# Seven products instead of eight in both up projections of a two-block kernel, with two weight sums formed in SBUF

## What is computed

```python
# first block
h = rms_norm(x, norm2_g[layer])
gate, val = jnp.split(h @ w_up[layer], 2, axis=-1)
gate = jax.nn.silu(causal_depthwise_conv(gate, ffn_dw_w[layer], ffn_dw_b[layer]))   # 3 taps over the tokens
x = x + (gate * val) @ w_down[layer]
# second block
v = rmsnorm(h, norm_ffn_w[l])
gate = causal_depthwise_conv_2(v @ w_gate[l], conv_w[l], conv_b[l])                   # 3 taps over the tokens
h = h + (jax.nn.silu(gate) * (v @ w_up[l])) @ w_down[l]
```

## Time and profile before

| | us |
|---|---|
| median of 3 runs | 1204.06 |
| the profiled execution | 1203.35 |
| its span | 1201.5 |
| TensorE busy | 1169.1 (97%) |
| VectorE busy | 688.9 (57%) |
| ScalarE busy | 560.1 (47%) |
| GpSimd busy | 531.6 (44%) |
| up projection of the first block, quads 2 to 11 | 254.4 to 472.0 |
| up projection of the second block, ten sevenfold blocks | 870.9 to 1072.4 |

### The profile page before, as it was taken

One profiled execution on the slowest core, in us unless ns is written; L12 is line 12 of the kernel. 1 busy time (PEld: TensorE's weight loads), 2 busy tenths in 40 slices (PEclk: granted clock), 3 DMA queues, 4 the chain that ended last, 5 costly groups with the idle time before them and its releaser, 6 DMA issues.

```text
span 1201.5 us, 17233 instructions
## 1 busy us (share of the span) xinstructions
PE 1169.1 (97%) x6948; PEld 976.3 (81%) x6948; DVE 688.9 (57%) x979; ACT 560.1 (47%) x881; POOL 531.6 (44%) x288
## 2 busy tenths in 40 slices
PE   7999999999999998999999999999899999999997
PEld 6877768788888886888877767778799999998886
DVE  5999973343332334444574577865956666674444
ACT  6356575333232323232445565655566665652323
POOL 3540033655545454445684220008445555564443
PEclk9999999999999998999989999999999999999999
DMA  5422021268978968867823120213255555642321
GB/s 181 140 78 96 4 70 35 71 231 226 236 242 207 243 234 209 201 243 203 207 57 113 64 71 28 80 37 106 70 169 182 182 187 178 191 162 83 105 89 70
DMA packets 115672, 167.75 MB, mean 140 GB/s; under 512 B 3363, under 2 KB 95882, under 8 KB 115594
## 3 DMA queue, kind: packets, MB, share of 16 engines
q1 hardware_dynamic: 102634, 120.26, 30.2%
q0 software_dynamic: 12800, 46.14, 16.0%
q10 hardware_dynamic: 160, 0.26, 0.1%
HBM read 164.29 MB, written 48.23 MB: 177 GB/s over the span
## 4 chain that ended last, share of the span: by engine, by line
PE 88%; DVE 5%; ACT 3%; issue 1%; POOL 1%; DMA 1%; POOLq 0%; ACTq 0%; DVEq 0%; SPq 0%
PE ps L2294 16%; PE ps L1960 13%; PE ps L1962 13%; PE ps L1961 13%; PE ps L2351 10%; PE ps L2355 10%; PE ps L2049 4%; PE ps L2539 3%; PE ps L2095 1%; DVE act_t L1508 1%; PE ps L2491 1%; PE ps L2080 1%; ACT w_hi L744 1%; PE ps L2410 1%; PE ps L2446 1%
## 5 line engine op out<-in xcount | busy, mean ns | idle before, releaser
L610 POOL TENSOR_TENSOR w_lo<-w_raw,w_hi 128x1024 fp32r<-128x1024 f32 x176 | 445.2, 2532 | 518.2 <-ACT w_hi L744 517.3
L744 ACT ACTIVATE w_hi<-w_raw 128x1024 fp32r<-128x1024 f32 x220 | 231.7, 1055 | 278.7 <-PE ps L1962 84.5
L1960 PE MATMUL ps<-h_hi,w_hi 128*128 128x512 f32 x656 | 261.7, 399 | 3.0 <-DVE h_lo L1347 2.1
L1961 PE MATMUL ps<-h_lo,w_hi 128*128 128x512 f32 x656 | 255.7, 390 | 0.0
L1962 PE MATMUL ps<-h_hi,w_lo 128*128 128x512 f32 x656 | 255.7, 390 | 0.0
L1558 DVE TENSOR_TENSOR tt<-act_t,tt 128x512 fp32r<-128x512 f32 x44 | 97.8, 2232 | 117.1 <-ACT tt L971 117.1
L1960 PEld LDWEIGHTS ps<-h_hi,w_hi 128*128 128x128 f32 x656 | 123.1, 188 | 36.3 <-issue 7.5
L1962 PEld LDWEIGHTS ps<-h_hi,w_lo 128*128 128x128 f32 x656 | 123.1, 188 | 26.2
L1961 PEld LDWEIGHTS ps<-h_lo,w_hi 128*128 128x128 f32 x656 | 123.2, 188 | 24.5 <-issue 0.5
L1565 DVE TENSOR_TENSOR ps<-ps,rbs 128x512 f32<-128x512 f32 x88 | 61.5, 698 | 120.2 <-PE ps L1962 118.9
L2294 PE MATMUL ps<-tt,w_hi 128*128 128x256 f32 x640 | 116.2, 283 | 0.0
(11 more groups left out here) (331 smaller groups left out, 1949.3 us busy)
## 6 DMA issues: line engine op xcount, KB each, us to landing
w_raw<-in_w_up SPq DMA_DIRECT2D x23, 1024.0 KB, 6.9
w_raw<-in_w_down SPq DMA_DIRECT2D x22, 1024.0 KB, 4.9
w_raw<-blocks SPq DMA_DIRECT2D x40, 512.0 KB, 3.6
w_raw<-in_w_in SPq DMA_DIRECT2D x19, 1024.0 KB, 5.1
blocks<-in_w_up POOLq DMA_DIRECT2D x12, 1408.0 KB, 10.5
blocks<-in_w_gate POOLq DMA_DIRECT2D x12, 1408.0 KB, 6.3
blocks<-blocks POOLq DMA_DIRECT2D x8, 1408.0 KB, 10.4
w_raw<-in_w_gate SPq DMA_DIRECT2D x20, 512.0 KB, 3.6
```

Source lines behind the costliest of these rows:

```text
L610: pool.tensor_tensor(unit_view(w_lo, at, flat), unit_raw(at, flat), unit_view(w_hi, at, flat).bitcast(F32), ALU.subtract).then_inc(s_lo, 1)
L744: act.activation(unit_view(w_hi, at, flat), unit_raw(at, flat), ACT.Copy).then_inc(s_hi, 1)
L1960: pe.matmul(ps[:, bank, :], whi, hi, start=first, stop=False, skip_group_check=True)
L1961: pe.matmul(ps[:, bank, :], whi, lo, start=False, stop=False, skip_group_check=True)
```

## The change

Both blocks now have one quad and ten sevenfold blocks. The buffer `blocks` and its 32 transfers go. Of the seven weights of a block, five are loaded. Position 3 and 4 are formed on VectorE in a new buffer `sum_raw` from loaded ones (`half_sum`). Of the five loaded, two (the products 0 and 6) are sums of two quarters: SP loads one quarter into `w_raw`, and GpSimd issues a DMA that adds the other onto it (`added`). The first block of each layer takes its products in the order 1, 2, 0, 3 and so on. The crossed activations are formed from eight gained tiles `xg` by four operations of 1024 elements on VectorE, all behind the variance. The first four units of the down projection are loaded one by one, and its first two k tiles take six banks before the last two.

```diff
-NC = (11, 1)
+NC = (1, 1)
...
 def on_vector(u):
-    return block_of(u) is not None and block_of(u)[1] in (1, 3, 5)
+    at = block_of(u)
+    return at is not None and at[1] in (1, 3, 5) and at not in ((0, 1), (NS[0], 1))
...
+def is_sum(u):
+    at = block_of(u)
+    return at is not None and at[1] in (3, 4)
+LOADED = [u for u in range(U_END) if not is_sum(u)]
...
+FIRST_ORDER = (1, 2, 0, 3, 4, 5, 6)
+def product_order(i, lay):
+    return FIRST_ORDER if i == NC[lay] else tuple(range(NB))
...
+        sum_raw = sb("sum_raw", [P, 2, DM])
...
-        blocks = nc.dram_tensor("blocks", (4, DK, DFF), F32, kind="Internal").ap()
...
         # SP: one_block
+                n = LOAD_AT[u]
+                before = LOADED[n - 4]
+                wait_lo(sp, before)
...
+                if block_of(before) is not None:
+                    g, at = block_of(before)
+                    j = order_of(g)[at]
+                    if j < 3:
+                        sp.wait_ge(s_sum, 2 * g + (2 if j == 2 else 1))
...
+                    halves = {0: val[0, 0:DK, v], 1: gate[0, 0:DK, n], 2: gate[0, DK:DM, n],
+                              5: val[0, DK:DM, v], 6: val[0, 0:DK, v]}
+                    for at, j in enumerate(product_order(i, lay)):
+                        if j in halves:
+                            one_block(u + at, halves[j])
...
         # GpSimd, behind each residue
+                    if u + 1 in FIRST_BLOCK:
+                        added(u + 1 + FIRST_ORDER.index(0))
+                    if block_of(u) is not None:
+                        g, at = block_of(u)
+                        if at == 2:
+                            added(u + 4)
+                        if at == 4 and g % NS[0] < NS[0] - 1:
+                            added(u + 3)
+            def added(u):
...
+                src = gate[0, 0:DK, c0:c0 + 256] if j == 6 else val[0, DK:DM, v0 + c0:v0 + c0 + 256]
+                wait_landed(pool, u)
+                pool.dma_start(unit_raw(u, True).rearrange("p (k n) -> p k n", k=KH),
+                               src.rearrange("(k p) n -> p k n", p=P), accum_op=ALU.add).then_inc(s_add[j // 6], 16)
...
         # ScalarE, between the units of the output projection
+            def gained(m, gcol):
+                act.activation(xg[:, m, :], xT[:, m, :], ACT.Copy, scale=par[:, 0, gcol + m:gcol + m + 1]).then_inc(s_xg, 1)
...
         # VectorE
+            def cross(lay, n):
+                b11, b12 = xg[:, 0:KH, 0:NH], xg[:, 0:KH, NH:SEQ]
...
+                    dve.tensor_tensor(t1f, b11, b12, ALU.subtract).then_inc(s_tf, 1)
...
+                def half_sum(i, n):
...
+                    if n == 0:
+                        wait_raw(dve, s1)
+                        wait_raw(dve, a11)
+                        if i > NC[lay]:
+                            wait_lo(dve, u - NB + 3)
+                        dve.tensor_tensor(unit_raw(u + 3, True), unit_raw(s1, True), unit_raw(a11, True),
+                                          ALU.add).then_inc(s_sum, 1)
+                    else:
+                        dve.wait_ge(s_sum, 2 * g + 1)
+                        wait_raw(dve, a12)
+                        if i > NC[lay]:
+                            wait_lo(dve, u - NB + 4)
+                        dve.tensor_tensor(unit_raw(u + 4, True), unit_raw(u + 3, True), unit_raw(a12, True),
+                                          ALU.add).then_inc(s_sum, 1)
...
         # VectorE, sevenfold
                     rest(u + 3)
+                    rest(u + 5)
                     for c in range(2):
...
-                        joined(c, 2, q1c, 2, left, CROSS)
-                    rest(u + 5)
+                        joined(c, 2, q1c, q1_at, left, CROSS)
+                    if not last:
+                        half_sum(i + 1, 0)
+                        half_sum(i + 1, 1)
...
         # TensorE, down
-                for k in range(KF - 2):
-                    ktile(u0 + k, k, first=(k == 0))
+                for ms in (range(6), range(6, KD)):
+                    for k in range(2):
+                        ktile(u0 + k, k, ms, first=(k == 0))
+                for k in range(2, KF - 2):
+                    ktile(u0 + k, k, range(KD))
```

More of the change, by code:

```diff
@@ L2280, in stream, with product @@
                     return h_hi[:, at, half], h_lo[:, at, half]
[L2282 removed]
+                def product(at, j, c):
                     bank = (SUM, ROW, CROSS, ROW, SUM, CROSS, ROW)[j][c]
[L2285 removed]
+                    whi, wlo = (quarter(w[:, (u + at) % 4, :]) for w in (w_hi, w_lo))
                     for k in range(KH):
@@ L2296, in product, with ready @@
                     mm.then_inc(s_q, 1)
-                wait_lo(pe, u)
-                if first:
-                    pe.wait_ge(s_tl, crossed + 1)
-                for c in range(2):
-                    if first:
+                def ready(j, c):
+                    if j == 0 and first:
+                        pe.wait_ge(s_tl, crossed + 1)
                         pe.wait_ge(s_gv, tiles + c - 1)
-                    else:
+                    elif j == 0:
                         pe.wait_ge(s_c, 8 * (g - 1) + 2 + c + 1)
-                    product(0, c)
@@ L2307, in sevenfold @@
-                wait_lo(pe, u + 1)
-                for c in range(2):
-                    if first:
+                    if j == 1 and first:
                         pe.wait_ge(s_conv, tiles + c - 1)
-                    else:
+                    elif j == 1:
                         pe.wait_ge(s_c, 8 * (g - 1) + 4 + 2 * c + 2)
-                    product(1, c)
-                wait_lo(pe, u + 2)
-                for c in range(2):
-                    if first and lay:
-                        pe.wait_ge(s_tc, 8)
-                    if not first:
-                        pe.wait_ge(s_c, 8 * (g - 1) + 4 + 2 * c + 1)
-                    product(2, c)
@@ L2334, in sevenfold @@
-                for c in range(2):
-                    pe.wait_ge(s_c, 8 * g + c + 1)
-                    product(5, c)
-                wait_lo(pe, u + 6)
-                for c in range(2):
-                    pe.wait_ge(s_qc, 8 * g + 4 + c + 1)
-                    product(6, c)
+                    if j == 2 and first:
+                        pe.wait_ge(s_rbs, lay + 1)
+                        if lay:
+                            pe.wait_ge(s_tc, 8)
+                    elif j == 2:
+                        pe.wait_ge(s_c, 8 * (g - 1) + 4 + 2 * c + 1)
@@ new lines, in ready @@
+                    if j == 3:
+                        if first:
+                            pe.wait_ge(s_tl, crossed + 2)
+                        pe.wait_ge(s_qc, 8 * g + (0 if first else 2) + c + 1)
+                    if j == 4:
+                        pe.wait_ge(s_qc, 8 * g + (2 if first else 0) + c + 1)
+                    if j == 5:
+                        if first:
+                            pe.wait_ge(s_tl, crossed + 3)
+                        pe.wait_ge(s_c, 8 * g + c + 1)
+                    if j == 6:
+                        if first:
+                            pe.wait_ge(s_tl, crossed + 4)
+                        pe.wait_ge(s_qc, 8 * g + 4 + c + 1)
@@ L2342, in down @@
+                for at, j in enumerate(product_order(i, lay)):
+                    wait_lo(pe, u + at)
+                    for c in range(2):
+                        ready(j, c)
+                        product(at, j, c)
             def down(lay, u0):
@@ L2357, in product, with ktile @@
                     return mm
-                def ktile(at, k, first=False):
+                def ktile(at, k, ms, first=False):
                     wait_lo(pe, at)
                     pe.wait_ge(s_alo, KF * lay + k + 1)
-                    for m in range(KD):
-                        if first and NS[lay]:
+                    for m in ms:
+                        if first:
                             done = 8 * (NS[0] * lay + NS[lay])
```

293 lines of the change are left out of this document (135 added, 158 removed).

## The result

| | before | after |
|---|---|---|
| median, us | 1203.97 (4 runs, 1203.62 to 1205.34) | 1297.72 (4 runs, 1291.38 to 1299.51) |
| ratio, 95% interval | | 1.0767 (1.0729 to 1.0805) |
| the profiled execution, its span | 1203.35, 1201.5 | 1296.67, 1294.9 |
| mean granted TensorE clock | 0.993 | 0.959 |

The changed kernel is 7.7% slower, 93.7 us; 52.5 were forecast, and the range ended at 1280. The page of the changed kernel: busy time, GpSimd's DMA queue, the shares of the chain that ended last, and the line of the first half sum.

The account below looks back on a forecast made before the run. TensorE was taken as the bound (busy 97% of the span, 88% of the chain), with new waits on VectorE's late joins. 1203.35 - 16.0 + 72.5 - 4 = 1255.9, 1256.5 against the median; range 1207 to 1280.

Parts of the forecast that it names:

- the signs of being wrong: Blocks at 20.16 us, half sums at 1.22 us throughout, or joins waiting for the transfer itself would refute the forecast.
- one point: In a block: whether both half sums end by t = 13.4, so taps end ahead of GpSimd's request at 18.5.
- the faster rival: Sums and S1 fit into VectorE's gap of 2.7 us, TensorE stays without gaps: 1184 us, chance 0.18.
- The matmuls, -16.0: First layer's up projection: ten quads become ten sevenfold blocks, each saving 1.60 us, -16.0 us.
- S1's landing is not on this loop as long as the add takes 4.4 to 7.3 us: In the sevenfold blocks: within those add times, the landing of summed weight S1 does not set the 24.2 us pace.
- The adding transfer: GpSimd's 512 KB add making S1: 5.1 us, scaled by bytes from 1408 KB adds; ends 3.6 and 10.5.
- its pace of 24.2: Late sevenfold blocks settle on a loop of held VectorE and GpSimd work: 24.2 us, 4.0 above 20.16; chance 0.5.
- the first has nothing before it: The first of each layer's ten sevenfold blocks inherits no stall; the other nine do.
- +72.5: Stalls in nine of ten sevenfold blocks of each layer: 18 x 4.03 = +72.5 us.
- The edges: Around the blocks, down projection starts and crossed sums: together -4 us, between -9 and +6.
- Late: Adds land late and the block pace follows: about 1317 us at 10.5 us, 1273 at 8; chance 0.08.
- Early: Adds land under 4.4 us, only the second sum is held, blocks 21.3 us: about 1210.5 us, chance 0.2.

Follow-up runs that it names:

- e1: The changed kernel without its 40 adding transfers (products 0 and 6 use one quarter of the weights), loads, VectorE sums and orders kept: 1205.36 us.
- e13: The changed kernel with S1 in its own raw buffer, loaded a block ahead, and second transfers that overwrite instead of adding: 1234.61 us.
- e6: The kernel before with eight sevenfold blocks in the first layer too, sums staged early in DRAM, second layer's staging moved: 1242.85 us, ratio 1.0328.
- e12: The kernel before with four sevenfold blocks in the first layer, their sums staged in 16 steps of 1024 KB before 170 us: 1196.27 us, ratio 0.9935.
- e9: The changed kernel, but SP starts the load following a half-loaded sum only once the adding transfer onto it has landed: 1365.02 us.
- e8: The changed kernel with the same transfers on GpSimd's queue overwriting instead of adding: 1240.71 us.
- e2: The changed kernel with a raw buffer of its own for each block's S1, its load going out a block earlier: 1270.53 us.
- e4: The changed kernel with S1's own buffer and S1's add issued behind GpSimd's residue of position 2 instead of 4: 1266.82 us.

## Why the prediction was wrong, step by step

**Direction: right, and the mechanism in part.** Slower was given 0.78, and what was to make it so came: the half sums wait for S1, GpSimd's residue gets ahead of the second, and VectorE's residue is held (1.2 us for each when free; 3.34 and 2.90 seen). But what set the pace was another loop, and its sign stood among the signs of being wrong: the joins wait for the transfer itself, as the 82.3 us of VectorE's idle time show. The held operations alone, without any transfer, cost little in a block (0.7 us in e1), and 29 us in all as soon as S1 comes a few us later (e13); that is the "one point" by which the faster rival was to be decided.

**The matmuls, -16.0: right.** e6's and e12's blocks show TensorE without gaps at the second layer's old pace, and four blocks gained 6.7 us for 6.4 forecast.

**The first step that failed** is the sentence "S1's landing is not on this loop as long as the add takes 4.4 to 7.3 us", with the 5.1 us and the 3.6 us under it. Both sizes were off, and the loop was another:

- *The adding transfer*, 5.1 forecast, took 7.3: 6.0 alone (e9), the rest for the loads beside it. The scaling by bytes from the adding transfers of 1408 KB gave too little, and the upper end of 10.5, time by rows of the matrix, too much. An overwriting transfer on the same queue took 4.1 (e8).
- *The load before it*, 3.6 forecast, took 6.66 in the loop above, since the gate quarter's load and the other add run in the same time.
- *The order.* The text did see that the load waits for VectorE's residue, but took S1's load as landed when GpSimd reaches the add. At its pace of 24.2 the two had seemed to fit between. With 3.1 and 2.1 us more they don't: held residue 2.9, load 6.7, add 7.2, half sums 4.5, joins and taps 5.1, 26.8 with the issues between. This loop holds no work of GpSimd's but the issue, and was in none of the rivals.
- *The clock.* The loop of the prediction counts TensorE's products at full clock. In six blocks the chain ran through one at half clock, some 14 us in all by the estimate above.

**The second step that failed** is "the first has nothing before it": the first block of each layer was put at no loss. It lost 10.7 and 7.6 us, mostly since the residues of its crossed activations stand behind the half sums of the second block in VectorE's queue (5.38 us of TensorE's waiting in the first layer). That is there without any transfer, too (8.3 and 5.7 us in e1).

**The numbers of the sum.** The blocks of both layers took 264.0 and 261.3 us against 201.8, which is +121.7 where +72.5 stood: 18.3 in the two first blocks, where nothing stood, and 103.4 in the others. The edges were -4, between -9 and +6; what is left is 93.4 (the difference of the spans) + 16.0 - 121.7 = -12.3. They show as 5.4 us from the last quad or block of the first layer to the end of its down projection, 6.1 from there to the second layer's blocks, and 0.7 behind the last block. Which part of the 6.1 is due to the crossed sums and which to the staging that is gone was not tried. So the blocks were 49.2 us too cheap and the edges 8.3 too dear.

**The rivals.** *Late* at 8 us was put at 1273; e2, with S1's load out of the way and its adds at 7.4 to 9.0, took 1270.5, with blocks of 24.7 us behind the first where 25.1 was put. Its arithmetic holds for the pace, and its chance of 0.08 was too small: the nearest row of an adding transfer said 10.5, and the text scaled it down by bytes alone. That the totals agree to 3 us is in part luck, since the first blocks and the edges are off in opposite directions. *Early* at 1210 is near e1's 1205.4, but e13, whose transfers land in 4.1 to 4.8 us, stands at 1234.6, between early and the main forecast: blocks behind the first take 22.8 us there, 2.6 above 20.16, where the early rival had 1.15 and the main forecast 4.0. *Faster* at 1184 has no run: even e1, without transfers, stands 21 us above it, 14 of them in the first blocks. The rule of the Trainium skill ("DMA: Bandwidth & Descriptors", the anatomy of one DMA on the GpSimd path), which gives an estimate of 3.2 us with no surcharge for adding, was rightly not followed: the trace doesn't agree with it for an add (6.0 alone, 7.3 in company), and 4.1 is 0.9 above it for the overwriting one, which had loads beside it.

**Smaller points.** The issue of an add takes GpSimd 1.3 us, not 1.04; in the earlier trace rows its residue from 900.92 ends at t = 12.5, not 12.3. The range's high end took late adds but not late loads with them.

## What to carry to other kernels

Where a buffer is freed, loaded, added onto and consumed within one step, write the loop down from release to release and set it against the pace: each transfer in it counts with what runs beside it, not as it lands alone. An adding transfer of another size is not priced by its bytes: 5.1 us by that way, 7.3 measured. Ask of the first turn of a loop what it holds that the others do not, and what now stands ahead of it in the queue. And a cheaper algorithm that needs prepared operands pays where they are prepared in stretches whose queues are empty: four more steps with seven products brought 6.7 us where their sums were staged early, and ten more, with the sums formed in the blocks of both layers, cost 94.

## What the runs showed of the hardware

- A DMA that adds onto SBUF, 512 KB in rows of 1 KB: 6.0 us alone (e9), 7.3 with loads beside it, 11.6 as the second of two adds issued together (e4). The same without addition: 4.1 (e8), but in 5760 packets instead of 21120 over the kernel. Loads beside adds slow down too: 6.8 for those of the gate quarter against 4.2 without second transfers (e1).
- A VectorE sum of two SBUF tensors (128x1024) that starts 0.1 us behind a GpSimd residue of that size takes 3.36 us instead of 1.23. Landing 0.7 us behind GpSimd's start cost both half sums (2.8 and 3.2 us, e13).
- Four adding transfers of 2560 KB in DRAM, issued together, keep a load of 1024 KB on the other queue from landing for 49 us; one of 1280 KB at a time (9.6 us) leaves the same loads at 5.6.
- The mean granted clock was 0.90 in the stretches where TensorE waited 2.6 to 5.2 us in nearly every block, and 1.00 in sevenfold blocks without such waits (e6). Behind a wait of 5.2 us it was 0.50 for 5.5 us, and 0.99 in the 11 us that followed. It followed the waits (without the transfers it is 0.989 over the span of e1), and gave some of them back where the next block's chain ran through the slow product.
